# Scan of 16-row blocks to 64x64 inverses: two of four heads sent crosswise through the matmul array, and powers plus the unit matrix in place of the additions

## The chip, the cores and the metric

One core of one Trainium2 chip. The metric is the device time of one execution in microseconds (us), of three runs the median.

## The reference, cut to what matters

The program is a whole two-block language-model layer in fp32 (norm, MLA attention with 8 heads, an RWKV-7 branch with a forward and a backward scan, gated merge, FFN; then a GLA block and a second FFN). The change touches only the RWKV-7 scans:

```python
def wkv7_scan(r, w, k, v, a, b, reverse):
    def step(state, inp):
        r_t, w_t, k_t, v_t, a_t, b_t = inp
        sa = jnp.einsum('bhvk,bhk->bhv', state, a_t)
        state = (state * w_t[:, :, None, :] + sa[..., None] * b_t[:, :, None, :]
                 + v_t[..., None] * k_t[:, :, None, :])
        return state, jnp.einsum('bhvk,bhk->bhv', state, r_t)
...
    fwd = direction(dlo_f, glo_f, w0[0], w2[0], g2[0], False)
    bwd = direction(dlo_b, glo_b, w0[1], w2[1], g2[1], True)
```

1024 steps, 8 heads of width 64, once forward and once backward.

## The kernel before

Each direction d (0 forward, 1 backward) walks 8 tiles i of 128 time steps. Within a tile the recurrence becomes matrix algebra: for every head a strictly triangular 128x128 matrix has to be inverted (I minus it). It is cut into halves of 64 steps, which lie on partitions 0 to 63 and 64 to 127 (`ROWS`), so that each head has two 64x64 triangles to invert. Four heads are worked on together (a group, `u` = 0 or 1): 8 tiles x 2 directions x 2 = 32 groups. Each triangle is cut into 16-row blocks; inside the blocks the inverse is the product (I+D)(I+D^2)(I+D^4)(I+D^8), and two further steps (H1/X5 with `G1`, H2/T64 with `G2`) put 16-row blocks together to 32 and 64. All operands are fp32; one fp32 matmul is two records in the trace (transposes are one).

**Steps of a group.** `scan_pe`, `scan_ve`, `scan_ae` and `scan_ge` are generators of TensorE, VectorE, ScalarE and GpSimd; each `yield` ends a step, and a group has 13 (`STEPS`). On PE: An (products of `ART` and `BT`; with four tiles of the array), D2, X2 and D4, X3 and D8, X4, H1, X5, H2, T64, V and Y, B, U, O and S; the masked products M go with the D2 and D8 steps (`kinds`). In D2 to H2 `diag` makes one 64x64 matmul per head and half, with operands and result in the same half: half 0 uses the array's quarter (rows 0-63, columns 0-63), half 1 the quarter (64-127, 64-127); the other two quarters have no work. Evacuation: ScalarE copies D2, D4, D8, H1; VectorE adds X2, X3, X4, X5 to the X before.

**Order.** `scans` interleaves the two scans and the attention of the other branch (`att_pe` and so on), one step of each in turn (a round), scan 0 being 7 steps ahead:

```python
s0, s1, at_ = scan(e, 0), scan(e, 1), att_and_loads()
for _ in range(7):
    next(s0)
    next(at_)
interleave(s0, s1, at_)
```

The attention's steps are the scores of a 128-row tile (two 96x128x512 matmuls into two PSUM banks; VectorE takes the maximum, ScalarE `Exp` at L1144, which frees the banks), the transposes of the tile before (eight, two banks), and every second time the product with v. After 64 tiles it is over and the two scans go on alone. All engines work their instructions in program order.

**PSUM.** Eight banks are handed out in a ring by `take`; a pair (`n=2`) begins at an even bank, and a bank is skipped for that if need be. Before PE writes a bank it waits for whoever read the bank's last contents (`frees`). A group takes An, Y, O as pairs and D2, four M, X2, D4, X3, D8, X4, H1, X5, H2, T64, V, B, U, S as single banks, 23 in all.

`state` (its matmuls are the ones with `lax`, L354) writes O and Y from the state matrix: 8 matmuls of 64x64 that go round all four quarters of the array.

Of the kernel before, what the change touches and what calls it, by code (L numbers as in the profile page):

```python
# [235 lines left out]
def program(nc, a, out):  # L236
    ctx = ExitStack()
    with ctx:
# [946 lines left out]
        def scan_memory(d):  # L1185
# [9 lines left out]
            def heads(n):  # L1195
                return part(n).rearrange("p (h n) -> p h n", h=4)
# [14 lines left out]
            c.D8, c.XA, c.XB = [heads(256) for _ in range(3)]  # L1211
# [16 lines left out]
        def hv(b, n=512):  # L1228
            return v3(ps[:, b, 0:n], 4)

        def two(b):

            return ps[:, b, :].rearrange("p (a h n) -> p a h n", a=2, h=4)
# [39 lines left out]
        def scan_pe(pe, d):  # L1273
# [9 lines left out]

            def kinds(i, u, q):
# [18 lines left out]
            for i in range(8):  # L1303
# [13 lines left out]
                for u in range(2):  # L1317
                    b = take(pe, PEs, "An", i, u, n=2)
                    pe.wait_ge(*at(VEs, "T", i, 2))
                    for q in range(2):  # L1320
                        p = 2 * u + q
                        for js in ROWS:
                            for n in range(2):
                                for j, rows in enumerate(ROWS):
                                    at_, bt = c.ART[rows, p, 0, js], c.BT[rows, p, js]
                                    x = mm(pe, ps[js, b + j, 128 * n + 64 * q:128 * n + 64 * q + 64], bt if n else at_,
                                           at_ if n else bt, True, True)
                    x.then_inc(*pe.sig(PEs, "An", i, u))
                    yield
                    b = take(pe, PEs, "D2", i, u)  # L1330
                    pe.wait_ge(*at(VEs, "D1", i, u, 1))
                    diag(b, 0, c.D1[:, 1], c.D1[:, 0])
                    diag(b, 256, c.D1[:, 0], c.D1[:, 1]).then_inc(*pe.sig(PEs, "D2", i, u))
# [19 lines left out]
                    b = take(pe, PEs, "X4", i, u)  # L1353
                    pe.wait_ge(*at(AEs, "D8", i, u))
                    pe.wait_ge(*at(VEs, "X3", i, u))
                    diag(b, 0, c.D8, c.XA).then_inc(*pe.sig(PEs, "X4", i, u))
                    yield
                    b = take(pe, PEs, "H1", i, u)
                    pe.wait_ge(*at(VEs, "X4", i, u))
                    pe.wait_ge(*at(GEs, "G2", i, u))  # L1360
                    for h in range(4):
                        for js in ROWS:
                            mm(pe, ps[js, b, 64 * h:64 * h + 64], c.X1[js, 1, h, :], ident[js, js], True, True)
                    diag(b, 256, c.G1, c.X1[:, 1]).then_inc(*pe.sig(PEs, "H1", i, u))
                    yield
                    b = take(pe, PEs, "X5", i, u)
                    pe.wait_ge(*at(AEs, "H1", i, u))
                    diag(b, 0, c.X1[:, 2], c.X1[:, 0])
                    diag(b, 256, c.X1[:, 0], c.X1[:, 2]).then_inc(*pe.sig(PEs, "X5", i, u))
                    yield  # L1370
                    b = take(pe, PEs, "H2", i, u)
                    pe.wait_ge(*at(VEs, "X5", i, u))
# [80 lines left out]
        def scan_ve(ve, d):  # L1453
# [11 lines left out]

            def less_own(i):
# [33 lines left out]
            for i in range(8):  # L1500
# [11 lines left out]
                for u in range(2):  # L1512
                    b = bank(PEs, "An", i, u)
                    ve.wait_ge(*at(PEs, "An", i, u))
                    for n, mask in enumerate((c.dN, c.dT)):
                        tt(ve, even_odd(c.D1[:, n]), ps[:, b:b + 2, 128 * n:128 * n + 128].rearrange("p j (q n) -> p j q n", q=2),
                           mask.unsqueeze(1).unsqueeze(1).broadcast_to([P, 2, 2, 64]), ALU.mult).then_inc(
                            *ve.sig(VEs, "D1", i, u, n))
                    yield
                    masked(i, u, 0)  # L1520
                    yield
                    ve.wait_ge(*at(PEs, "X2", i, u))
                    tt(ve, c.XB, hv(bank(PEs, "X2", i, u), 256), c.XA, ALU.add).then_inc(*done("X2", i, u))
                    yield
                    ve.wait_ge(*at(PEs, "X3", i, u))
                    ve.wait_ge(*at(VEs, "X2", i, u))
                    tt(ve, c.XA, hv(bank(PEs, "X3", i, u), 256), c.XB, ALU.add).then_inc(*done("X3", i, u))
                    masked(i, u, 1)
                    yield
                    ve.wait_ge(*at(PEs, "X4", i, u))  # L1530
                    tt(ve, c.X1[:, 1], hv(bank(PEs, "X4", i, u), 256), c.XA, ALU.add).then_inc(*done("X4", i, u))
                    yield
                    yield
                    ve.wait_ge(*at(PEs, "X5", i, u))
                    tt(ve, c.X2, two(bank(PEs, "X5", i, u)), c.X1[:, 0:2], ALU.add).then_inc(*done("X5", i, u))
# [4 lines left out]
                    ve.wait_ge(*at(VEs, "X5", i, u))  # L1540
# [25 lines left out]
        def scan_ae(ae, d):  # L1566
# [6 lines left out]

            def exps(i):
# [11 lines left out]
            for i in range(8):  # L1586
# [1418 lines left out]
```

## Time and profile before

| | |
|---|---|
| median of 3 runs | 3591.54 us (3588.69 to 3591.72) |
| profiled execution | 3593.16 us, span 3591.4 us |
| PE (matmuls) busy | 3414.7 us, 95% of the span |
| VectorE, ScalarE, GpSimd busy | 1714.2, 1107.4, 324.1 us |
| scans beside the attention | about 573 to 1185 us of the span |
| scans alone | about 1185 to 1341 us |

The span is the time between the first and the last recorded instruction; the execution's own time is 1.8 us more. A line number like L355 is that of a helper (L355: every plain matmul, L354: matmuls of `state` and `rows_by`, L358: transposes, L361: ScalarE copies, L364: VectorE and GpSimd operations on two tensors), so groups are told apart by the names of the tiles. Scan 0's tiles lie in AR and EX, scan 1's in X, W and AR; `HT` and `W` also hold the attention's.

### The profile page before, as it was taken

To read this page: it belongs to the slowest core of one execution; us is meant where nothing else is said; L and a number is where in the kernel's file an instruction comes from. 1 tells how busy PE (TensorE), PEld (TensorE's weight loads), DVE (VectorE), ACT (ScalarE), POOL (GpSimd) and SP (SyncE) were. 2 spreads that over 40 slices of the span, in tenths; PEclk is the share of its full clock that TensorE was granted. 3 is DMA by queue.
4 is the path that set the end of the run, shared out by engine and by line. 5 is a ranking of instruction groups with operands and counts; after the bars stand their busy time and mean duration, and the time that the engine had idled before them with its cause. 6 is when DMAs were issued, how large, how long until landed. Compare 5 with 4: busy or idle time off the path is not lost.

```text
span 3591.4 us, 61000 instructions
## 1 busy us (share of the span) xinstructions
PE 3414.7 (95%) x27176; PEld 2714.1 (76%) x27176; DVE 1714.2 (48%) x2528; ACT 1107.4 (31%) x1797; POOL 324.1 (9%) x342
## 2 busy tenths in 40 slices
PE   8989999999999996999999999899899999999998
PEld 7678776777777883487888888687677788888877
DVE  4353555665555566554335434552454522352235
ACT  4323324444444330132124212433232311241124
POOL 1232241111111222000000000001000000000000
PEclk9999999999999998999999999999899999999999
DMA  3241252212111204421112211232003111121113
GB/s 138 70 143 50 83 187 81 66 39 63 38 58 46 100 12 144 139 90 42 47 47 94 77 47 47 100 107 96 18 30 106 65 53 47 59 100 59 47 65 106
DMA packets 89974, 269.82 MB, mean 75 GB/s; under 512 B 11552, under 2 KB 12080, under 8 KB 89712
## 3 DMA queue, kind: packets, MB, share of 16 engines
q1 hardware_dynamic: 78960, 230.26, 19.6%
q0 software_dynamic: 10752, 35.66, 2.9%
q8 instruction: 215, 3.52, 0.4%
q14 instruction: 47, 0.39, 0.0%
HBM read 219.73 MB, written 46.14 MB: 74 GB/s over the span
## 4 chain that ended last, share of the span: by engine, by line
PE 83%; DVE 10%; ACT 3%; issue 2%; DMA 1%; SPq 0%; POOL 0%; DVEq 0%; ACTq 0%
PE ps L355 78%; PE ps L354 3%; PE ps L358 2%; DVE SM L375 2%; DVE X L364 2%; DVE AR L364 1%; ACT HT L1144 1%; DVE HT L368 1%; DVE W L364 1%; ACT WS L361 0%; DVE HL L364 0%; ACT W L2043 0%; DVE EX L364 0%; DVE WS L364 0%; DMA qk_d<-AR 0%
## 5 line engine op out<-in xcount | busy, mean ns | idle before, releaser
L355 PE MATMUL ps<-HH,WS 128*128 128x512 f32 (+1 forms) x3232 | 1000.6, 391 | 0.0
L355 PEld LDWEIGHTS ps<-HH,WS 128*128 128x128 f32 (+1 forms) x3232 | 607.2, 188 | 129.7
L355 PE MATMUL ps<-HL,WS 128*128 128x512 f32 x1616 | 639.1, 395 | 7.1 <-DVE HL L364 6.9
L364 DVE TENSOR_TENSOR WS<-W,WS 128x1024 fp32r<-128x1024 f32 x244 | 299.4, 1227 | 635.1 <-ACT WS L361 635.1
L361 ACT ACTIVATE WS<-W 128x1024 fp32r<-128x1024 f32 x244 | 256.6, 1052 | 891.8 <-PE ps L355 885.1
L355 PE MATMUL ps<-WS,SA 128*128 128x512 f32 x2112 | 491.3, 394 | 24.6 <-DVE SA L364 22.4
L355 PEld LDWEIGHTS ps<-WS,SA 128*128 128x128 f32 x2112 | 400.9, 191 | 112.1 <-issue 26.8
L355 PEld LDWEIGHTS ps<-HL,WS 128*128 128x128 f32 x1616 | 303.8, 188 | 73.0 <-issue 7.6
L355 PE MATMUL ps<-AR 64*64 64x64 f32 (+2 forms) x4928 | 202.3, 241 | 10.0 <-ACT AR L361 4.2
L355 PE MATMUL ps<-HL,HI 128*128 128x512 f32 (+1 forms) x512 | 208.3, 407 | 3.7 <-POOL WL L364 2.8
L355 PE MATMUL ps<-WS,HH 128*128 128x512 f32 x640 | 203.7, 394 | 7.5 <-DVE HL L364 5.4
L364 DVE TENSOR_TENSOR SA<-HA,SA 128x512 fp32r<-128x512 f32 x176 | 120.9, 691 | 184.8 <-ACT SA L361 184.8
L355 PE MATMUL ps<-WS,HL 128*128 128x512 f32 x576 | 206.9, 392 | 0.8 <-DVE X L364 0.8
L355 PE MATMUL ps<-HH,HI 128*128 128x512 f32 (+1 forms) x512 | 205.6, 401 | 0.0
L355 PE MATMUL ps<-HH,WL 128*128 128x512 f32 (+1 forms) x512 | 204.6, 400 | 0.0
L355 PEld LDWEIGHTS ps<-AR 64*64 64x64 f32 (+1 forms) x4928 | 161.7, 135 | 56.7 <-issue 35.6
L361 ACT ACTIVATE SA<-HA 128x512 fp32r<-128x512 f32 x176 | 110.3, 631 | 281.7 <-PE ps L355 252.9
L355 PE MATMUL ps<-HT 96*128 96x512 f32 (+1 forms) x384 | 187.0, 619 | 0.6 <-DMA HT<-v_d 0.5
L361 ACT ACTIVATE AR<-ps 128x512 f32<-128x512 f32 (+4 forms) x240 | 115.3, 493 | 130.2 <-PE ps L355 92.0
L364 DVE TENSOR_TENSOR HA<-HA,ps 128x512 f32<-128x512 f32 x88 | 60.4, 687 | 184.9 <-PE ps L355 184.1
L355 PEld LDWEIGHTS ps<-WS,HH 128*128 128x128 f32 x640 | 120.8, 189 | 33.7 <-issue 5.6
L1144 ACT ACTIVATE HT<-ps,SM 128x1024 f32<-128x1024 f32 x64 | 71.3, 1114 | 214.7 <-DVE SM L368 214.7
(287 smaller groups left out, 4442.1 us busy)
## 6 DMA issues: line engine op xcount, KB each, us to landing
W<-in_w_fd SPq DMA_DIRECT2D x88, 512.0 KB, 3.3
AR<-rw_d SPq DMA_DIRECT2D x104, 256.0 KB, 4.0
W<-in_w_fg SPq DMA_DIRECT2D x44, 512.0 KB, 3.3
W<-in_w_fu SPq DMA_DIRECT2D x44, 512.0 KB, 3.3
W<-in_w_tok SPq DMA_DIRECT2D x24, 512.0 KB, 3.3
rw_d<-X POOLq DMA_DIRECT2D x40, 256.0 KB, 3.3
X<-in_x SPq DMA_DIRECT2D x16, 512.0 KB, 5.5
W<-in_w_g SPq DMA_DIRECT2D x16, 512.0 KB, 3.7
```

What stands on the lines that cost most here:

```text
L354: return pe.e.matmul(o, l, r, start=start, stop=stop, skip_group_check=True)
L355: return pe.e.matmul(o, l, r, start=start, stop=stop)
L358: return pe.e.transpose(o, i, ident)
L361: return e.e.activation(o, x, ACT.Copy)
L364: return e.e.tensor_tensor(o, x, y, op)
L368: return e.e.tensor_scalar(o, x, s1, None, o1)
L375: return e.e.tensor_reduce(o, x, AX.X, op)
L1144: ae.e.activation(APB[i % 2], ps[:, b:b + 2, :].rearrange("p a b -> p (a b)"), ACT.Exp, bias=sm(264 + i % 4, 1), scale=SCALE, accum_out=sm ...
```

## The change

`cross` takes the place of `diag` from D2 to X5. Heads 0 and 1 stay in their halves; of heads 2 and 3 the operands of half z give a result in half 1-z, in a bank of its own. So each of these steps now writes two banks and its matmuls go round all four quarters; heads 2 and 3 change halves at every step, and the step pattern is such that operands meet in the same half. For this An makes a third product for heads 2 and 3 into the other half (4 more matmuls a group), and VectorE masks it into `XA` (`D1`, 2).

X + D X is computed as (I + D) X: VectorE makes `DI` = D + I from the D2, D4, D8 results (`and_one`), PE multiplies with `DI`, and the X results are copied by ScalarE. `D8` alone is no longer kept. H1's addition goes the same way (`X1[2]` = product + I), so that X5 needs no addition. As both engines read the same bank, VectorE's `and_one` waits for ScalarE's copy of the same step (of the last copy from these banks). GpSimd's addition for `XA` is two instructions of half the size.

Per group the matmuls number 20 instead of 16 in An, and 96 in D2 to X5 as before (16+8+16+8+8+8+16+16 before; 16+24+16+8+16+16 now), all 96 crosswise. The banks: An, D2, D4, D8, X4, H1, X5, Y, O as pairs and four M, H2, T64, V, B, U, S as single ones, 28 a group, besides those that are skipped.

```diff
+            def cross(b, c0, lhs, rhs):
+
+                for m in range(2):
+                    for h in (m, 2 + m):
+                        for z in range(2):
+                            o = ROWS[1 - z if h > 1 else z]
+                            x = mm(pe, ps[o, b + h // 2, c0 + 64 * m:c0 + 64 * m + 64], lhs[ROWS[z], h, :], rhs[ROWS[z], h, :],
+                                   True, True)
                 return x
...
-                        for js in ROWS:
-                            for n in range(2):
+                        for n in range(2 + q):
+                            for z, js in enumerate(ROWS):
                                 for j, rows in enumerate(ROWS):
...
-                    b = take(pe, PEs, "X2", i, u)
+                    b = take(pe, PEs, "D4", i, u, n=2)
                     pe.wait_ge(*at(AEs, "D2", i, u))
+                    cross(b, 0, c.D2[:, 1], c.D2[:, 0])
+                    cross(b, 128, c.D2[:, 0], c.D2[:, 1])
                     pe.wait_ge(*at(GEs, "X", i, u))
-                    diag(b, 0, c.D2[:, 0], c.XA).then_inc(*pe.sig(PEs, "X2", i, u))
-                    b = take(pe, PEs, "D4", i, u)
-                    diag(b, 0, c.D2[:, 1], c.D2[:, 0])
-                    diag(b, 256, c.D2[:, 0], c.D2[:, 1]).then_inc(*pe.sig(PEs, "D4", i, u))
-                    yield
-                    b = take(pe, PEs, "X3", i, u)
+                    pe.wait_ge(*at(VEs, "D2", i, u))
+                    cross(b, 256, c.DI, c.XA).then_inc(*pe.sig(PEs, "D4", i, u))
+                    yield
+                    b = take(pe, PEs, "D8", i, u, n=2)
                     pe.wait_ge(*at(AEs, "D4", i, u))
-                    pe.wait_ge(*at(VEs, "X2", i, u))
-                    diag(b, 0, c.D4[:, 0], c.XB).then_inc(*pe.sig(PEs, "X3", i, u))
-                    b = take(pe, PEs, "D8", i, u)
-                    diag(b, 0, c.D4[:, 1], c.D4[:, 0]).then_inc(*pe.sig(PEs, "D8", i, u))
+                    cross(b, 0, c.D4[:, 1], c.D4[:, 0])
+                    pe.wait_ge(*at(VEs, "D4", i, u))
+                    cross(b, 128, c.DI, c.XB).then_inc(*pe.sig(PEs, "D8", i, u))
                     kinds(i, u, 1)
...
+            def and_one(nm, i, u, o, c0):
+
+                ve.wait_ge(*at(PEs, nm, i, u))
+                ve.wait_ge(*at(AEs, {"D4": "X2", "D8": "X3"}.get(nm, nm), i, u))
+                tt(ve, in_pairs(o), heads_of(bank(PEs, nm, i, u), c0), cst["I64"].unsqueeze(1).unsqueeze(1).broadcast_to([P, 2, 2, 64]),
+                   ALU.add).then_inc(*done(nm, i, u))
...
-                    copy(c.D4, two(bank(PEs, "D4", i, u)), "D4", i, u)
-                    yield
-                    copy(c.D8, hv(bank(PEs, "D8", i, u), 256), "D8", i, u)
-                    yield
-                    yield
-                    copy(c.X1[:, 0::2], two(bank(PEs, "H1", i, u)), "H1", i, u)
-                    yield
+                    both(c.D4, "D4", i, u)
+                    one(c.XB, "X2", "D4", 256, i, u)
+                    yield
+                    one(c.XA, "X3", "D8", 128, i, u)
+                    yield
+                    copy(in_pairs(c.X1[:, 1]), heads_of(bank(PEs, "X4", i, u), 0), "X4", i, u)
+                    yield
+                    one(c.X1[:, 0], "H1", "H1", 0, i, u)
+                    yield
+                    both(c.X2, "X5", i, u)
                     yield
```

How the instructions stand. First ScalarE while the scans are alone, from the copy of scan 0's H2 to the next copies of scan 1's H1. Before (scan 0: `AR 128x256` H2, `EX` V, Y, U, O; scan 1: `AR 128x2x2x64` An, `X 128x512` D2 and D4, `AR 128x256` D8, `AR 128x2x256` H1):

```order
L361 ACTIVATE AR<-ps 128x256
L361 ACTIVATE AR<-ps 128x2x2x64
L361 ACTIVATE X<-ps 128x512
L361 ACTIVATE EX<-ps 64x256
L361 ACTIVATE EX<-ps 128x2x2x64
L361 ACTIVATE X<-ps 128x512
L361 ACTIVATE AR<-ps 128x256
L361 ACTIVATE EX<-ps 128x256
L361 ACTIVATE EX<-ps 128x2x2x64
L361 ACTIVATE AR<-ps 128x2x256
```

The same place of the change (`X 128x2x2x128` are D2 and D4, the two `AR 128x256` together XB and XA, the next `AR 128x256` X4, the last H1):

```order
L361 ACTIVATE AR<-ps 128x256
L361 ACTIVATE AR<-ps 128x2x2x64
L361 ACTIVATE X<-ps 128x2x2x128
L361 ACTIVATE EX<-ps 64x256
L361 ACTIVATE EX<-ps 128x2x2x64
L361 ACTIVATE X<-ps 128x2x2x128
L361 ACTIVATE AR<-ps 128x256 x2
L361 ACTIVATE EX<-ps 128x256
L361 ACTIVATE AR<-ps 128x256
L361 ACTIVATE EX<-ps 128x2x2x64
L361 ACTIVATE AR<-ps 128x256
```

The copy of D8 is gone, those of XB, XA and X4 have come, and H1's copy is half as wide.

Second VectorE, scan 0's first group beside the attention. Before (`128x2x2x64` the masks of An, `128x512` the masks of M, `128x256 x2` X2 and X3; the rows between are the attention's):

```order
L364 TENSOR_TENSOR AR<-ps,CS 128x2x2x64 x2
L364 TENSOR_TENSOR AR<-ps,CS 128x512 x2
L1119 RECIPROCAL SM<-SM 128x1
L368 TENSOR_SCALAR HT<-HT,SM 128x1024
L375 TENSOR_REDUCE SM<-ps 128x1
L368 TENSOR_SCALAR SM<-SM 128x1
L364 TENSOR_TENSOR AR<-ps,AR 128x256 x2
L364 TENSOR_TENSOR AR<-ps,CS 128x512 x2
```

and with the change:

```order
L364 TENSOR_TENSOR AR<-ps,CS 128x2x2x64 x2
L364 TENSOR_TENSOR AR<-ps,CS 128x128
L364 TENSOR_TENSOR AR<-ps,CS 128x256
L364 TENSOR_TENSOR AR<-ps,CS 128x512 x2
L1119 RECIPROCAL SM<-SM 128x1
L368 TENSOR_SCALAR HT<-HT,SM 128x1024
L375 TENSOR_REDUCE SM<-ps 128x1
L368 TENSOR_SCALAR SM<-SM 128x1
L364 TENSOR_TENSOR AR<-ps,CS 128x256 x2
L364 TENSOR_TENSOR AR<-ps,CS 128x512 x2
```

One small mask has come, and an `and_one` (`AR<-ps,CS 128x256`) now stands ahead of the masks of M as well.

## Rows read from the trace of the kernel before

**Rows 1.** The page's first parts: span, and busy time of each engine

```profile
span 3591.4 us, 61000 instructions
PE 3414.7 (95%) x27176; PEld 2714.1 (76%) x27176; DVE 1714.2 (48%) x2528; ACT 1107.4 (31%) x1797; POOL 324.1 (9%) x342
```

**Rows 2.** Busy time by stretch: scans with attention, scans alone

```profile
core 0: us, PE busy (x) PEld busy (x) DVE busy (x) ACT busy (x) POOL busy (x), PEclk, DMA share, GB/s
573.00:1185.00 612.00, 583.27 (x11140) 456.36 (x11138) 363.89 (x683) 256.04 (x542) 93.55 (x111) 1.00 0.16 50
1185.00:1341.00 156.00, 146.80 (x4045) 133.40 (x4040) 94.69 (x187) 52.61 (x114) 35.39 (x42) 1.00 0.19 64
```

**Rows 3.** Timeline of PE: `state`, then X4 of scan 1 (`diag`)

```profile
start us, us, engine line op out<-in xcount [idle before <-releaser]
760.37 0.46 PE L354 MATMUL ps<-EX,AR 64*64 64x64 f32 x16
...
761.84 0.68 PE L355 MATMUL ps<-AR 64*64 64x64 f32 x16
```

**Rows 4.** What PE waited for, 573 to 1185 us

```profile
engine line waited for: us in total, times, longest us
PE ps L355 <- ACT AR L361: 7.7, 7, 1.6
PE ps L358 <- ACT W L361: 4.5, 4, 1.4
PE ps L358 <- ACT EX L361: 4.3, 5, 0.9
PE ps L355 <- ACT HT L1144: 2.9, 5, 0.6
```

**Rows 5.** Timeline, one round of scores and its release

```profile
1039.53 1.98 PE L355 MATMUL ps<-HT 96*128 96x512 f32 x4
...
1041.55 1.23 DVE L375 TENSOR_REDUCE SM<-ps 128x1 f32<-128x1024 f32 x1 [1.55 <-PE ps L355]
...
1042.81 0.15 DVE L368 TENSOR_SCALAR SM<-SM 128x1 f32<-128x1 f32 x1
...
1043.00 1.11 ACT L1144 ACTIVATE HT<-ps,SM 128x1024 f32<-128x1024 f32 x1 [2.76 <-DVE SM L368]
...
1043.67 1.24 PE L358 MATMUL ps<-CS,HT 128*128 128x128 f32 x8
...
1044.10 0.37 ACT L361 ACTIVATE AR<-ps 128x256 f32<-128x256 f32 x1
...
1044.26 0.42 PEld L358 LDWEIGHTS ps<-CS,HT 128*128 128x128 f32 x4 [0.17 <-ACT HT L1144]
```

**Rows 6.** Groups of instructions by form, 573 to 1341 us

```profile
line engine op names shapes xcount | busy us, mean ns | idle before us <-releasers
L361 ACT ACTIVATE AR<-ps 128x512 f32<-128x512 f32 x75 | 44.7, 597 | 43.4 <-PE ps L355 37.6 <-PE ps L358 5.8
L361 ACT ACTIVATE AR<-ps 128x256 f32<-128x256 f32 x93 | 35.0, 383 | 39.7 <-PE ps L355 22.1 <-DVE X L364 8.9 <-DVE AR L364 8.6
L364 DVE TENSOR_TENSOR AR<-ps,AR 128x256 f32<-128x256 f32 x93 | 39.2, 422 | 68.8 <-PE ps L355 68.8
L364 DVE TENSOR_TENSOR X<-ps,AR 128x512 f32<-128x512 f32 x7 | 4.8, 692 | 4.4 <-PE ps L355 4.4
L364 DVE TENSOR_TENSOR EX<-ps,EX 128x128 f32<-128x128 f32 x16 | 4.6, 288 | 14.8 <-PE ps L354 14.8
L364 POOL TENSOR_TENSOR AR<-AR,CS 128x256 f32<-128x256 f32 x77 | 56.9, 761 | 153.8 <-DVE AR L364 151.3 <-ACT AR L361 2.0
```

**Rows 7.** Timeline, scans alone: H1, its copy, then X5 and more

```profile
1242.45 0.68 PE L355 MATMUL ps<-CS,AR 64*64 64x64 f32 x16
1242.97 1.16 PE L355 MATMUL ps<-AR 64*64 64x64 f32 x48
...
1243.65 0.60 ACT L361 ACTIVATE AR<-ps 128x512 f32<-128x512 f32 x1 [1.08 <-PE ps L355]
...
1244.39 2.95 PE L355 MATMUL ps<-AR 64*64 64x64 f32 x80 [0.26 <-ACT AR L361]
```

More of the change, by code:

```diff
@@ L1210, in scan_memory @@
             c.An, c.G1, c.G2 = [heads(256) for _ in range(3)]
-            c.D8, c.XA, c.XB = [heads(256) for _ in range(3)]
+            c.DI, c.XA, c.XB = [heads(256) for _ in range(3)]
+            c.eye = cst["I64"].unsqueeze(1).broadcast_to([P, 4, 64])
             c.X1, c.X2 = pair(3), pair(2)
@@ L1229, in hv, with crossed, heads_of, in_pairs @@
             return v3(ps[:, b, 0:n], 4)
-        def two(b):
-            return ps[:, b, :].rearrange("p (a h n) -> p a h n", a=2, h=4)
+        def crossed(b, c0, n=128):
+            return ps[:, b:b + 2, c0:c0 + n]
+        def heads_of(b, c0):
+            return crossed(b, c0).rearrange("p g (m n) -> p g m n", m=2)
+        def in_pairs(ap):
+            return ap.rearrange("p (g m) n -> p g m n", g=2)
         def by_parity(b):
@@ L1329, in scan_pe @@
                     yield
-                    b = take(pe, PEs, "D2", i, u)
+                    b = take(pe, PEs, "D2", i, u, n=2)
                     pe.wait_ge(*at(VEs, "D1", i, u, 1))
-                    diag(b, 0, c.D1[:, 1], c.D1[:, 0])
-                    diag(b, 256, c.D1[:, 0], c.D1[:, 1]).then_inc(*pe.sig(PEs, "D2", i, u))
+                    cross(b, 0, c.D1[:, 1], c.D1[:, 0])
+                    cross(b, 128, c.D1[:, 0], c.D1[:, 1]).then_inc(*pe.sig(PEs, "D2", i, u))
                     pe.wait_ge(*at(AEs, "T", i, 3))
@@ L1355, in scan_pe @@
-                    pe.wait_ge(*at(VEs, "X3", i, u))
-                    diag(b, 0, c.D8, c.XA).then_inc(*pe.sig(PEs, "X4", i, u))
+                    b = take(pe, PEs, "X4", i, u, n=2)
+                    pe.wait_ge(*at(AEs, "X3", i, u))
+                    pe.wait_ge(*at(VEs, "D8", i, u))
+                    cross(b, 0, c.DI, c.XA).then_inc(*pe.sig(PEs, "X4", i, u))
                     yield
-                    b = take(pe, PEs, "H1", i, u)
-                    pe.wait_ge(*at(VEs, "X4", i, u))
+                    b = take(pe, PEs, "H1", i, u, n=2)
@@ L1360, in scan_pe @@
+                    pe.wait_ge(*at(AEs, "X4", i, u))
+                    cross(b, 0, c.X1[:, 1], c.eye)
                     pe.wait_ge(*at(GEs, "G2", i, u))
[L1361 to L1364, printed above, removed]
+                    cross(b, 128, c.G1, c.X1[:, 1]).then_inc(*pe.sig(PEs, "H1", i, u))
@@ L1365, in scan_pe @@
                     yield
-                    b = take(pe, PEs, "X5", i, u)
+                    b = take(pe, PEs, "X5", i, u, n=2)
                     pe.wait_ge(*at(AEs, "H1", i, u))
-                    diag(b, 0, c.X1[:, 2], c.X1[:, 0])
-                    diag(b, 256, c.X1[:, 0], c.X1[:, 2]).then_inc(*pe.sig(PEs, "X5", i, u))
+                    pe.wait_ge(*at(VEs, "H1", i, u))
+                    cross(b, 0, c.X1[:, 2], c.X1[:, 0])
+                    cross(b, 128, c.X1[:, 0], c.X1[:, 2]).then_inc(*pe.sig(PEs, "X5", i, u))
@@ L1572, in copy, with both, one @@
                 cp(ae, o, x).then_inc(*ae.sig(AEs, nm, i, u, frees=(PEs, nm, i, u)))
+            def both(o, nm, i, u):
+                ae.wait_ge(*at(PEs, nm, i, u))
+                cp(ae, o.rearrange("p a (g m) n -> p g a (m n)", g=2),
+                   crossed(bank(PEs, nm, i, u), 0, 256).rearrange("p g (a k) -> p g a k", a=2)).then_inc(
+                    *ae.sig(AEs, nm, i, u, frees=(PEs, nm, i, u)))
+            def one(o, nm, of, c0, i, u):
+                ae.wait_ge(*at(PEs, of, i, u))
+                cp(ae, in_pairs(o), heads_of(bank(PEs, of, i, u), c0)).then_inc(
+                    *ae.sig(AEs, nm, i, u, frees=(PEs, of, i, u)))
             def exps(i):
@@ L1593, in scan_ae @@
                 for u in range(2):
-                    ae.wait_ge(*at(VEs, "D1", i, u, 1))
+                    ae.wait_ge(*at(VEs, "D1", i, u, 2))
                     copy(even_odd(c.An), by_parity(bank(PEs, "An", i, u)), "An", i, u)
                     yield
-                    copy(c.D2, two(bank(PEs, "D2", i, u)), "D2", i, u)
+                    both(c.D2, "D2", i, u)
                     yield
@@ L1647, in scan_ge @@
                 for u in range(2):
-                    ge.wait_ge(*at(VEs, "D1", i, u, 1))
-                    tt(ge, c.XA, c.D1[:, 1], bc(cst["I64"], 4), ALU.add).then_inc(*ge.sig(GEs, "X", i, u))
+                    ge.wait_ge(*at(VEs, "D1", i, u, 2))
+                    for g, src_ in enumerate((c.D1[:, 1, 0:2, :], c.XA[:, 2:4, :])):
+                        x = tt(ge, c.XA[:, 2 * g:2 * g + 2, :], src_, bc(cst["I64"], 2), ALU.add)
+                    x.then_inc(*ge.sig(GEs, "X", i, u))
                     ge.wait_ge(*at(AEs, "An", i, u))
```

25 lines of the change are left out of this document (11 added, 14 removed).

## Prediction

> **What bounds the kernel now.** I read the page first [rows 1]: PE is busy for 95% of the span, every other engine for less than half. Only work that leaves PE's stream, or time in which PE waits, can move the end. All the change touches lies between about 573 and 1341 us, so I then read that stretch in its two parts [rows 2]: with the attention PE is busy for 583 of 612 us, alone for 147 of 156 us; the other engines have room (ScalarE 256 of 612, VectorE 364 of 612). The busy share hides two things, and the next views show them. First, PE's pace: 16 records of `state`, which goes round four quarters of the array, take 0.46 us, 16 records of a `diag` step, which uses two, take 0.68 us [rows 3]. Less the 0.22 us that the last record itself takes, that is 0.016 and 0.031 us a record. Second, how near PE already is to waiting: beside the attention the waits add up to some 28 us over all rows of that view, the longest four of which are shown [rows 4], and where scans run alone X5 waited 0.26 us for the copy of H1 [rows 7]. So PE bounds, with little slack behind it.
>
> **What the change takes away.** 96 matmuls a group x 32 groups x 2 records = 6,144 records go from two quarters to four: 6,144 x 0.0147 us (the difference of the two paces, [rows 3]) = 90 us. An's 4 more matmuls are 256 records x 0.016 = 4 us more; its new order rotates through the quarters a little better, so I take +3. On PE alone: **-87 us**.
>
> What I weigh against it is a rule of the Trainium skill. The row shows one `state` block of 8 matmuls, two of them on each quarter and neighbours sharing row half or column half, at half of `diag`'s time per record. The skill's page "TensorE: Matmul & The Clock Gate" (Part 3, packing small matmuls) says that a weight load overlaps matmuls in flight only where the row group differs. By that rule two quarters on the same row half would not overlap, the 90 us would be nil, and this is a rival below. The trace disagrees with it as far as `state` goes.
>
> **What it puts on the other engines.** VectorE: before, three additions of 0.42 us and one of 0.69 us a group, 1.95 us; now four `and_one` of 0.42 and one mask of 0.29 us, 1.97 us [rows 6]: nothing. ScalarE: three copies of 0.60 and one of 0.38, 2.18 us; now three of 0.60 and four of 0.38, 3.32 us [rows 6]: 1.14 us a group more, 25 us in the attention's stretch, where it is idle for 356 us: hidden as a sum, not as a place in line. GpSimd: one addition of 0.76 us becomes two, which lie between half of that and the whole; they have 2 us and more until D4's third product reads them, so nothing, and if PE came to them early at most 0.4 us a group. DMAs and their queues are not touched.
>
> **What becomes late.** Four places; the first two are large.
>
> (a) The release of the scores' banks. From the end of the score matmuls (1041.5 us) to the end of `Exp` (1044.1) 2.6 us pass: reduce 1.23, scale 0.15, Exp 1.11 and the hand-overs [rows 5]. Here PE had been held at the transposes' second half already (0.17 us). With 23 banks a group the ring comes back to one of the scores' banks after 2.2 to 3.9 us of PE work, 3.3 us in the middle (counted along the code, matmuls x pace). With 28 banks, skipped ones, and the work halved in those steps, it is 1.5 to 3.4 us, 2.2 in the middle: nearly every one of the 64 score blocks is now short, by 0.5 us on average, 30 us in all against 3. Where scan 0's next step comes first, it also wants ScalarE, and its copy stands behind the Exp: it is ready 3.0 us (0.37 or 0.60 more) after the scores, on top of about 2.3 us of work, so short by 0.8 to 0.9. That holds for half of the 60 rounds: 28 us; the other half wait for the bank, 24 us. Together 52 us, where now it is some 25 us. **+27 us**.
>
> (b) O and S. By the new ring, in 17 of the 32 groups S takes a bank that O, right ahead of it, has just filled, and waits for ScalarE's copy of O: the last matmul 0.22, the copy 0.38 and hand-overs, 0.7 us. In the others there is mostly another step between. 17 x 0.7 = **+12 us**; before, this pair never met.
>
> (c) Scans alone. The longest wait of a step was copy or addition; now D4 to D8 is copy 0.60, copy 0.38, `and_one` 0.42, with tail and hand-overs 1.8 us from PE's end to the second half of D8, and the other scan covers 0.9 to 1.4 us of it and D8's first half 0.23. H1 to X5 is 1.1 us against 0.5 to 0.9 of cover, An to D2 1.0 against 0.5 to 0.9, X4 to H1 0.65 against 0.3. The shortfalls of a pair of groups (one of each scan) add up to 2.8 us, against 1.8 us now (156 less 147 us over five pairs, [rows 2]). For five pairs: **+5 us**.
>
> (d) VectorE in the attention's rounds. `and_one` now waits for a ScalarE copy that stands behind Exp, so scan 1's VectorE step and the next reduce stand behind it. Between nothing (PE has other work) and 0.42 + 0.38 us for each of 60 rounds, 48 us. I take **+8 us**, near the lower end, since rounds with the transposes and with the product with v follow and have 1.0 and 1.9 us of PE work of their own.
>
> Sum: -87 + 27 + 12 + 5 + 8 = -35 us, against the profiled execution of 3593.2 us: 3558 us. That execution lies 1.6 us above the median; taken off, **3556 us**, 1.0% faster.
>
> The skill's page "TensorEngine Tiling (Array Packing)" (PSUM Bottleneck) warns that tiling speeds up TensorE and not the evacuation. The trace can't show that for this change yet; (a) and (b) are what it would mean here.
>
> **Rivals.**
>
> R1: the waits are hidden. If VectorE and ScalarE keep up, -70 to -87 us, 3505 to 3521 us. For it: both engines are idle for most of the time [rows 2]. Against it: they are idle because they wait in line, and PE is already held by Exp in the row shown [rows 5]. Chance 0.13.
>
> R2, slower: the chain through Exp, copy and `and_one` becomes the clock of the attention's stretch. Price: (d) at its upper end, 48 us, and in addition the same queueing once more at each D8 and X5 of the stretch, 22 groups x 2 x 1.0 us (0.60 + 0.42) = 44 us; -87 + 27 + 12 + 5 + 48 + 44 = +49 at most, +5 to +30 us likely, 3597 to 3622 us. It decides from the point where a round's PE work beside the scores (2.8 us) is below the 4.2 us that Exp, copy and `and_one` take for the late cases in more than one round out of two and a half. Chance 0.10.
>
> R3: four quarters are no faster in these steps than two. Then the 90 us are nil and the longer chains remain, as the cover is as before, some +5 to +15 us, 3597 to 3607 us. Against it stands the pace of `state` [rows 3]. The skill's rule quoted above would give this. Chance 0.04.
>
> R4: gain and waits cancel, 3585 to 3598 us. Chance 0.10.
>
> **The numbers.** My forecast, with (a) to (d) between half and one and a half of what I take, gives -9 to -61 us, 3531 to 3583 us, chance 0.63. The range reaches half into R1 and into R4: 3517 to 3592. About 0.2% (7 us) is what a measurement of this kernel can tell from no change. Faster by more: 0.63 + 0.13 and a little of R4, 0.80; same: 0.07; slower: 0.13.
>
> **What would show it.** PE's records for D2 to X5 should stand 0.015 us apart, 16 in 0.46 us; their busy time in the two stretches falls together by 50 to 90 us. PE's waits for ScalarE (L1144 and L361) beside the attention should come to 60 to 90 us instead of 28. S should wait for the copy of O in half the groups. The stretch alone should be near 130 us instead of 156, the one with the attention near 600 instead of 612. I am wrong if the records stand 0.03 apart (R3), if the waits stay below 40 us (R1), or if the stretch with the attention gets longer (R2).

## The result and the profile after

The changed kernel takes 3617.21 us, median of 4 runs (3612.48 to 3624.22), beside 3591.63 us for the kernel before on the same chip. The ratio is 1.0073, with a 95% interval of 1.0051 to 1.0094: 0.7% slower, 26 us. The forecast was 3556 us, and the range (to 3592) does not hold the result; rival R2 had the size, and part of the mechanism.

The first parts of the page of the changed kernel, answering to [rows 1]:

```profile
span 3611.8 us, 61777 instructions
PE 3366.4 (93%) x27432; PEld 2645.9 (73%) x27432; DVE 1707.3 (47%) x2560; ACT 1141.4 (32%) x1893; POOL 330.3 (9%) x374
```

PE is busy for 48 us less, and yet the span of this execution is 20 us longer. To see where, I cut the scans' stretch at the places where the attention and the scans end. They are 1185.7 and 1351.7 us before, 1219.4 and 1377.8 us after: 26.1 us are lost by the end of the scans (behind it this execution runs 6 us shorter). The part with the attention is 34 us longer, the scans alone are 8 us shorter (158 against 166 us). That the part with the attention gets longer is the sign which the prediction had set for R2. Busy time by stretch, of the kernel before (as [rows 2], up to the end of the scans):

```profile
core 0: us, PE busy (x) PEld busy (x) DVE busy (x) ACT busy (x) POOL busy (x), PEclk, DMA share, GB/s
563.00:1352.00 789.00, 748.73 (x15475) 604.75 (x15476) 467.89 (x888) 316.26 (x672) 130.65 (x154) 1.00 0.17 52
```

The same of the changed kernel, whole and in its two parts:

```profile
core 0: us, PE busy (x) PEld busy (x) DVE busy (x) ACT busy (x) POOL busy (x), PEclk, DMA share, GB/s
563.00:1378.00 815.00, 705.79 (x15723) 540.97 (x15724) 459.87 (x919) 350.06 (x769) 136.57 (x185) 0.96 0.16 50
...
573.00:1219.00 646.00, 558.26 (x11331) 416.78 (x11331) 360.74 (x706) 280.41 (x610) 98.02 (x134) 0.97 0.16 48
1219.00:1368.00 149.00, 131.17 (x4128) 111.70 (x4124) 90.26 (x195) 61.83 (x142) 37.19 (x51) 0.98 0.20 65
```

The length less PE's busy time is its idle time: 789 - 748.7 = 40 us before, 815 - 705.8 = 109 us now. So **69 us of idle time** have come for 43 us less of work. And PEclk, the granted clock, is 0.96 where it was 1.00. Three things are to be explained: the matmuls' gain, the waits, the clock.

**The matmuls are faster, nearly as forecast.** Timeline of PE in the changed kernel, X5 of scan 0, all 16 matmuls (32 records) crosswise:

```profile
1049.02 0.69 PE L355 MATMUL ps<-AR 64*64 64x64 f32 x32 [2.25 <-DVE AR L364]
```

0.69 less the last record's 0.22 is 0.47 us for 32 records, 0.015 us a record; in [rows 3] `diag` needed 0.031. From the start of a block's first record to that of its last (medians over the blocks at full clock without a wait), D2 falls from 0.93 to 0.48 us, X2 and D4 together from 1.34 to 0.71, X3 and D8 together from 0.88 to 0.48, X4 from 0.46 to 0.24, H1 and X5 from 0.93 to 0.48 each: 2.6 us a group, less 0.05 for An, about **82 us** in 32 groups. The rule of the Trainium skill ("TensorE: Matmul & The Clock Gate", Part 3), by which a weight load overlaps only where the row group differs, does not hold here. In `diag` as in `cross` (and in `state`) each matmul stands on the other row half than the one before, so by that rule the two would keep the same pace. They do not: with the column halves changing too, a record takes half the time. The prediction says that neighbours in `state` share a row half or a column half; by the code they never share a row half.

**The waits.** What PE waited for, 563 to 1378 us, the longest rows:

```profile
engine line waited for: us in total, times, longest us
PE ps L358 <- ACT HT L1144: 18.0, 21, 2.6
PE ps L355 <- DVE AR L364: 16.6, 34, 2.3
PE ps L354 <- ACT EX L361: 14.1, 9, 2.4
PE ps L355 <- ACT AR L361: 13.1, 12, 2.0
PE ps L354 <- ACT W L361: 12.5, 8, 3.4
PE ps L354 <- ACT HT L1144: 7.0, 4, 1.8
PE ps L355 <- ACT HT L1144: 5.3, 6, 1.2
```

Against [rows 4] three kinds are new. L1144 (Exp) holds the scores' banks; `EX L361` and `W L361` at L354 are S waiting for the copy of O, 9 and 8 times, 17 in all; `DVE AR L364` is mostly X5 and D8 waiting for `and_one`. Followed through the program step by step, PE's waits for semaphores come to 124 us against 47: for Exp 34.5 against 5.5 us, S for O's copy 28.0 against none, X5 for H1's `and_one` 11.4 against none. This count comes out above PE's idle time; the view, which counts idle time alone, gives 109 against 41 us, for Exp 30.3 against 5.4, for S 26.6.

How S waits is seen in one round. Timeline, changed kernel: scores, O, then S:

```profile
start us, us, engine line op out<-in xcount [idle before <-releaser]
1007.12 1.98 PE L355 MATMUL ps<-HT 96*128 96x512 f32 x4
...
1009.03 0.69 PE L354 MATMUL ps<-EX,AR 128*64 128x64 f32 x16
1009.14 1.23 DVE L375 TENSOR_REDUCE SM<-ps 128x1 f32<-128x1024 f32 x1 [0.50 <-PE ps L355]
1010.40 0.15 DVE L368 TENSOR_SCALAR SM<-SM 128x1 f32<-128x1 f32 x1
1010.59 1.11 ACT L1144 ACTIVATE HT<-ps,SM 128x1024 f32<-128x1024 f32 x1 [2.96 <-DVE SM L368]
...
1011.70 0.37 ACT L361 ACTIVATE EX<-ps 128x256 f32<-128x256 f32 x1
1012.12 0.20 PEld L354 LDWEIGHTS ps<-EX,AR 128*64 128x64 f32 x4 [2.54 <-ACT EX L361]
```

O is done at 1009.7, ScalarE is idle, and still the copy comes only at 1011.70. It stands behind Exp in ScalarE's program, and Exp waits for VectorE's maximum. S, right behind O on PE, waits 2.4 us here, where I had counted 0.7.

X5's wait has the same root. Timeline, changed kernel, scores, then H1's evacuation:

```profile
1045.43 1.21 DVE L375 TENSOR_REDUCE SM<-ps 128x1 f32<-128x1024 f32 x1
...
1046.87 1.11 ACT L1144 ACTIVATE HT<-ps,SM 128x1024 f32<-128x1024 f32 x1 [4.66 <-DVE SM L368]
...
1047.97 0.37 ACT L361 ACTIVATE AR<-ps 128x256 f32<-128x256 f32 x1
...
1048.45 0.42 DVE L364 TENSOR_TENSOR AR<-ps,CS 128x256 f32<-128x256 f32 x1 [1.62 <-ACT AR L361]
```

Maximum, Exp, copy, `and_one`, then X5 (1049.02, the row above): four instructions on two engines in line.

**The clock.** Busy time by stretch of the changed kernel around the wait of S shown above, which ended at 1012.12:

```profile
1008.00:1012.00 4.00, 1.72 (x19) 0.74 (x17) 2.02 (x3) 1.41 (x3) 0.00 (x0) 1.00 0.02 4
1012.00:1016.00 4.00, 3.88 (x60) 3.69 (x61) 1.86 (x3) 1.49 (x4) 2.56 (x2) 0.63 0.00 0
1016.00:1020.00 4.00, 4.00 (x76) 3.59 (x75) 2.15 (x4) 1.63 (x4) 1.04 (x1) 0.94 0.14 50
```

Within 1 us of the wait's end the granted clock falls to its lower level (1.2 GHz) for some 3.4 us. In the scans' stretch this happens 14 times, 58 us in all; in the kernel before once, 7 us, at its end. 13 of the 14 begin within 1.4 us of the end of a wait of 1.8 us or more, most of them behind it and two 0.2 to 0.3 us ahead of it. Ten other waits of over 1.7 us have none behind them.

### The profile page after: what moved, and what is told of

It reads as the page before. It is cut to its first block, busy times and chain, and to the rows that moved or that the text cites. A ratio compares the mean times of both kernels' runs of the same rounds, so it can differ in the third digit from the quotient of the medians.

```text
span 3611.8 us, 61777 instructions
## 1 busy us (share of the span) xinstructions
PE 3366.4 (93%) x27432; PEld 2645.9 (73%) x27432; DVE 1707.3 (47%) x2560; ACT 1141.4 (32%) x1893; POOL 330.3 (9%) x374
## 4 chain that ended last, share of the span: by engine, by line
PE 76%; DVE 13%; ACT 6%; issue 3%; DMA 1%; SPq 0%; POOL 0%; DVEq 0%; ACTq 0%
PE ps L355 72%; DVE SM L375 3%; PE ps L354 3%; DVE X L364 2%; DVE AR L364 2%; PE ps L358 2%; ACT HT L1144 2%; DVE HT L368 1%; ACT AR L361 1%; ACT WS L361 0%; DVE W L364 0%; ACT W L2081 0%; DVE WS L364 0%; DVE HL L364 0%; DMA qk_d<-AR 0%
## 5 line engine op out<-in xcount | busy, mean ns | idle before, releaser
L364 DVE TENSOR_TENSOR WS<-W,WS 128x1024 fp32r<-128x1024 f32 x244 | 299.6, 1228 | 632.5 <-ACT WS L361 632.5
L361 ACT ACTIVATE WS<-W 128x1024 fp32r<-128x1024 f32 x244 | 256.8, 1053 | 887.0 <-PE ps L355 880.3
L364 DVE TENSOR_TENSOR SA<-HA,SA 128x512 fp32r<-128x512 f32 x176 | 120.9, 692 | 184.8 <-ACT SA L361 184.8
L361 ACT ACTIVATE SA<-HA 128x512 fp32r<-128x512 f32 x176 | 110.6, 632 | 281.4 <-PE ps L355 252.7
L364 DVE TENSOR_TENSOR AR<-ps,CS 128x256 f32<-128x256 f32 (+2 forms) x256 | 112.0, 469 | 184.2 <-ACT AR L361 172.5
L355 PE MATMUL ps<-AR 64*64 64x64 f32 (+2 forms) x5568 | 168.8, 243 | 27.5 <-DVE AR L364 16.6
L355 PEld LDWEIGHTS ps<-AR 64*64 64x64 f32 (+1 forms) x5568 | 120.7, 137 | 81.9 <-issue 39.7
L361 ACT ACTIVATE AR<-ps 128x256 f32<-128x256 f32 (+4 forms) x304 | 131.1, 448 | 131.4 <-PE ps L355 82.5
L364 DVE TENSOR_TENSOR HA<-HA,ps 128x512 f32<-128x512 f32 x88 | 60.5, 688 | 184.2 <-PE ps L355 183.4
```

The costliest lines, as they stand in the source:

```text
L355: return pe.e.matmul(o, l, r, start=start, stop=stop)
L361: return e.e.activation(o, x, ACT.Copy)
L364: return e.e.tensor_tensor(o, x, y, op)
```

## The experiments

"Slow" is the time at the lower clock. Ratios are to the kernel before on the same chip (4 runs of it beside the changed kernel, 11 to 23 beside the others, median 3591.6 to 3594.0 us); the experiments ran on several chips, so small differences between them are better read from the ratios. The other columns are of one profiled execution each. Length, busy and idle are PE's from 563 us to the end of the scans, slow and the waits for the same stretch.

| kernel | median us | ratio, 95% | length | busy | idle | slow | S for O | for Exp |
|---|---|---|---|---|---|---|---|---|
| before | 3591.6 | | 789 | 749 | 40 | 7 | 0 | 5.5 |
| changed | 3617.2 | 1.0051-1.0094 | 815 | 706 | 109 | 58 | 28.0 | 34.5 |
| e1 | 3651.7 | 1.0152-1.0178 | 853 | 775 | 78 | 34 | 26.3 | 19.7 |
| e2 | 3626.8 | 1.0082-1.0108 | 825 | 765 | 60 | 37 | 23.8 | 18.7 |
| e3 | 3603.4 | 1.0018-1.0042 | 806 | 706 | 100 | 65 | 0 | 35.5 |
| e4 | 3606.5 | 1.0024-1.0050 | 805 | 722 | 83 | 34 | 26.1 | 24.6 |
| e5 | 3616.5 | 1.0044-1.0069 | 813 | 757 | 56 | 17 | | |
| e6 | 3600.6 | 1.0008-1.0025 | 797 | 730 | 67 | 21 | | |
| e7 | 3594.5 | 0.9997-1.0015 | 799 | 721 | 78 | 48 | | |
| e8 | 3623.2 | 1.0067-1.0091 | 821 | 776 | 45 | 27 | | |
| e9 | 3578.6 | 0.9949-0.9977 | 780 | 726 | 54 | 21 | | |
| e10 | 3588.0 | 0.9973-0.9994 | 783 | 711 | 72 | 31 | | |
| e11 | 3589.0 | 0.9976-1.0001 | 785 | 713 | 72 | 31 | | |
| e12 | 3610.8 | 1.0039-1.0066 | 807 | 753 | 54 | 14 | 0 | |
| e13 | 3618.9 | 1.0057-1.0081 | 816 | 725 | 91 | 54 | 8.4 | |
| e14 | 3639.1 | 1.0114-1.0140 | 830 | 727 | 103 | 68 | 28.0 | |
| e15 | 3620.0 | 1.0062-1.0088 | 818 | 774 | 44 | 14 | 6.4 | |

### e1: no crossing, all else as changed

```diff
-                            o = ROWS[1 - z if h > 1 else z]
+                            o = ROWS[z]
```
(and the same in An's third product)

> The changed kernel with every head kept in its own half: the same matmuls, banks, copies and waits, but D2 to X5 on two quarters. Where PE's time alone counts it is 70 to 90 us slower than the changed kernel's 3617 us. If the waits that came with the change (PE waits 124 us in the scans' stretch, 47 before) fill up what the faster matmuls save, the slow matmuls cover these waits again: waits of 50 to 70 us, the clock at full speed in the stretch, and a time within 20 us of the changed kernel's. If four quarters gave nothing in place, the time and the waits would both be the changed kernel's.

3651.7 us, 34 us slower than the changed kernel and 60 us slower than the one before. That lies between the two cases expected, and the clock did not stay at full speed (34 us slow). So crossing by itself is a gain, but of 34 us. PE's busy time, less half of the slow time, is 758 us here and 677 us in the changed kernel: 81 us of work go, and idle time rises from 78 to 109 us, slow time from 34 to 58 us. Banks, chain and An's third product together cost 60 us. Of the 26 us of busy time that e1 has more than the kernel before, 14 are the clock and 4 An; some 9 us are left. In part they are the ends of matmuls, which count as busy when PE stops behind them: PE stops 97 times here, 58 times in the kernel before (pauses over 0.06 us).

### e2: the kernel before with the banks of the change

```diff
-                    b = take(pe, PEs, "D2", i, u)
+                    b = take(pe, PEs, "D2", i, u, n=2)
```
(and the same for X4, H1, X5)

> The kernel before, with D2, X4, H1 and X5 taken as pairs of banks, so the ring goes on 28 banks a group instead of 24; nothing else. If the pressure on the banks is what costs (terms a and b), the waits for Exp's and O's banks grow by 10 to 25 us and the time goes to 3600 to 3617 us. If it is the chain of copies and additions, or the clock, it stays within 5 us of 3592 us.

No instruction is added, and the kernel is 35 us slower, more than the 8 to 25 us expected. What PE waited for in e2, 563 to 1388 us:

```profile
PE ps L354 <- ACT EX L361: 14.1, 9, 2.4
PE ps L355 <- ACT AR L361: 9.3, 11, 1.6
PE ps L354 <- ACT W L361: 8.4, 8, 1.9
PE ps L355 <- ACT HT L1144: 6.9, 9, 1.4
```

The first and third row are S, again 17 times. And PE's busy time has grown by 16 us at the same instructions:

```profile
563.00:1388.00 825.00, 764.94 (x15474) 616.89 (x15474) 468.73 (x887) 320.27 (x674) 130.69 (x154) 0.98 0.16 50
```

That is the clock: 30 us more at half speed than in the kernel before, half of which is 15 us. Idle time (+20) and clock (+16) make up the 36 us of the stretch.

### e3 and e4: one cause taken out of the changed kernel

```diff
                     b = take(pe, PEs, "U", i, u)
+                    bs_ = plan.next_place(BANKS, (PEs, "S", i, u))[1]
...
-                    b = take(pe, PEs, "S", i, u)
+                    b = bs_
+                    for tok in plan.releases((PEs, "S", i, u)):
+                        pe.wait_ge(*tok)
```

> The changed kernel, with the bank of S taken right behind that of U in the ring, so it is never the one that O has just filled. The 28 us of waits of S for the copy of O go. If such waits lie on the path one for one, the time falls by 20 to 30 us to 3587 to 3597 us, more if the half-speed stretches get rarer. If they only delay what would wait later anyway (the next step for Exp or a copy), it falls by under 10 us.

3603.4 us, 14 us faster, less than the 28 us of the wait. Slow time did not fall (65 against 58 us), and 4 of the 13 falls stand behind no wait of 1.7 us or more. A new wait takes part of the old one's place: the shifted ring brings H1 to O's banks, 8 times, 10.5 us, most of this row (in the changed kernel it had 4.0 us):

```profile
PE ps L355 <- ACT EX L361: 13.6, 7, 2.0
```

In e4 PE adds I and X itself, and `and_one` is gone:

```diff
+            def plus(b, c0, lhs, rhs, one_):
...
+                    for k, l_, r_ in ((0, lhs, rhs), (1, c.eye, one_)):
...
-                    pe.wait_ge(*at(VEs, "D2", i, u))
-                    cross(b, 256, c.DI, c.XA).then_inc(*pe.sig(PEs, "D4", i, u))
+                    plus(b, 256, c.D2[:, 0], c.XA, c.XA).then_inc(*pe.sig(PEs, "D4", i, u))
```
(and so for X3, X4 and the second product of H1)

> The changed kernel, with I and X added by PE into PSUM (8 more small matmuls on I in X2, X3, X4 and H1, 32 a group) and no and_one: one ScalarE copy ends each step. PE has 32 x 32 x 2 records x 0.015 us = 30 us more. If VectorE's place behind the copy (and_one) is what costs, waits of PE for D4, D8, H1 fall by 15 to 25 us, the attention's reduce comes earlier, and the time is within 15 us of 3617 us or below it. If it is not, the time is 20 to 35 us longer: 3637 to 3652 us.

3606.5 us: 11 us faster, though PE has about 30 us more to do (busy time +16 us, with 24 us less at half speed). The chain is a cost of its own.

### e5: the chain without the banks

The changed kernel's steps with `diag`'s layout: D2, D8, X4, H1, X5 write one bank each, nothing crosses.

> The changed kernel's chain (and_one behind ScalarE's copy, X copied) without crossing and without its banks: D2, D8, X4, H1, X5 in one bank each, 23 banks a group. If the banks (+35 us by e2) and the chain add up to the 60 us that e1 lost against the kernel before, the chain alone costs 25 us: 3610 to 3625 us. If the chain costs only where the banks are late as well, it is within 8 us of 3592 us.

3616.5 us, 23 us above the median of the kernel before beside it. By the ratios e2 costs 34, e5 20 and e1 59 us: banks and chain are two costs that nearly add. The largest rows of what PE waited for in e5 (its helper lines stand two further down):

```profile
PE ps L357 <- DVE AR L366: 10.9, 17, 1.9
PE ps L357 <- ACT AR L363: 10.2, 12, 1.5
```

### e6 to e8: fewer banks, less crossing, both remedies

e6 crosses D2 and D4 alone and takes 24 banks; e7 is e3 and e4 together; e8 is e7 with e6's banks. e8 does not give the right result: part of its additions of I and X is missing from it. Its instructions are all there, so its time can be read; two sums are open in one bank at the same time, but no run shows that this is why.

> The changed kernel with crossing in D2 and D4 alone; D8, X4, H1, X5 stay in their halves and take one bank each, so 24 banks a group as before the change. Faster matmuls by 32 x 1.0 us = 32 us only, instead of 75. If the four banks more are what turns the gain into a loss, this comes below the changed kernel: about 3617 - 35 + 43 = 3625 us if banks cost the full 35 us, less if waits shrink with the shorter ring as well; under 3592 us only if the chain's 25 us are hidden too. If banks did not matter it would be 3617 + 40 = 3657 us.

> e3 and e4 together: crossing everywhere, PE adds I and X in PSUM, no and_one, and S's bank is taken behind U's. If the two gains (14 and 11 us) are of different waits they add: 3588 to 3596 us. If one wait only takes the place of the other, it stays at 3600 to 3607 us.

> As e7, but with crossing in D2 and D4 alone and one bank each for D8, X4, H1, X5: 24 banks a group. PE has 43 us more than e7. If the banks' pressure is worth over 43 us it is faster than e7, otherwise 0 to 40 us slower; the waits for Exp's banks should fall from some 25 to under 10 us either way, and the clock stay at full speed in the stretch.

e6 is 17 us faster than the changed kernel, though it gives up some 43 us of faster matmuls: idle time 67 instead of 109 us, slow time 21 instead of 58. It was expected at about 3625 us, so the shorter ring gives back more than the 35 us that e2 had cost. e7 has both gains (23 us against 25 for the sum) and stands level with the kernel before. e8 is 29 us slower than e7, the second of the two cases expected. Idle time fell by 33 us and slow time by 21, but PE's busy time rose by 55: besides the products, PE's own additions then run on two quarters as well, which the expectation left out. With `and_one` gone the faster matmuls are worth more than the banks.

### e9: cross only where no chain grows

The kernel before, with the change in An, D2, D4 and X2 only. From X3 on `diag` and VectorE's additions are back.

```diff
+                    bx = take(pe, PEs, "X3", i, u)
+                    b = take(pe, PEs, "D8", i, u)
                     pe.wait_ge(*at(AEs, "D4", i, u))
-                    cross(b, 0, c.D4[:, 1], c.D4[:, 0])
-                    pe.wait_ge(*at(VEs, "D4", i, u))
-                    cross(b, 128, c.DI, c.XB).then_inc(*pe.sig(PEs, "D8", i, u))
+                    diag(b, 0, c.D4[:, 1], c.D4[:, 0]).then_inc(*pe.sig(PEs, "D8", i, u))
+                    pe.wait_ge(*at(AEs, "X2", i, u))
+                    diag(bx, 0, c.D4[:, 0], c.XB).then_inc(*pe.sig(PEs, "X3", i, u))
```

> The kernel before with crossing only where no chain gets longer: An, D2 and D4 with X2 cross (one and_one, behind D2); from X3 on everything is as before the change, VectorE's additions too. 25 banks a group by the ring (before 24). PE has 32 x (0.38 + 0.63) - 2 = 30 us less. If banks and chain were what ate the gain, most of the 30 us is kept: 3562 to 3580 us. If any faster matmul in this stretch is given back in waits, whatever the banks and the chain, it is 3585 to 3600 us.

3578.6 us, ratio 0.9963 (0.9949 to 0.9977): **faster than both**. Of 30 us of faster matmuls 13 to 15 are kept (by the ratio and by the medians). Its row:

```profile
563.00:1343.00 780.00, 725.72 (x15723) 576.30 (x15724) 468.58 (x919) 327.16 (x707) 135.34 (x185) 0.99 0.17 53
```

Against the kernel before: busy -23, idle +14 (this execution lies 5.5 us above its median). What PE waited for shows what is left of the banks' cost:

```profile
PE ps L355 <- ACT AR L361: 12.4, 14, 2.0
PE ps L358 <- ACT HT L1144: 6.1, 12, 0.8
PE ps L354 <- ACT HT L1144: 5.2, 4, 1.8
```

> e9, and H1 and X5 cross too, with I added by PE in H1 (no and_one) and both evacuated by ScalarE: two banks more (27). PE has 32 x 0.62 = 20 us less than e9, two pairs more of banks cost up to 20 us. Theory of banks: within 10 us of e9. Theory of waits in proportion to PE's gain: the same. Without a cost of banks: 3545 to 3560 us.

> e10 with the bank of S taken behind U's. Where S meets O's banks in e10, 5 to 15 us faster than e10; where it doesn't, the same, or slower if the shifted ring brings O and another step together, as H1 in e3.

e10 is 8 to 9 us slower than e9: two pairs of banks more, and H1's and X5's evacuation by ScalarE, cost more than crossing H1 and X5 gives. These two costs were not separated. S's place (e11) changes nothing. e10 and e11 have 15 and 13 us less busy time than e9, and 18 us more idle time each.

### e12: e2 with e3's edit

> e2 (the kernel before with 28 banks a group) with the bank of S taken behind U's: it splits e2's 35 us. S waited 24 us for O's copy in e2. If that is the larger part, this is 15 to 25 us below e2's 3627 us; if the waits only move to the next step that meets O or Exp, under 8 us below it.

16 us below e2: somewhat less than half of the banks' cost is S's wait, with the clock behind it. Most of it is the clock. Idle time falls by 6 us only (60 to 54), as H1 now waits for O's banks, five times 1.9 us; slow time falls from 37 to 14 us. Behind those five waits the clock falls once, while in e2 it fell behind six of S's seven waits of 1.8 to 2.4 us.

### e13 to e15: is it the waits that pull the clock down?

```diff
-                    b = take(pe, PEs, "S", i, u)
+                    b = plan.next_place(BANKS, (PEs, "S", i, u))[1]
+                    if b in (bo, bo + 1):
+                        for n in range(24):
+                            mm(pe, ps[ROWS[n % 2], bu, 64 * (n % 8 // 2):64 * (n % 8 // 2) + 64],
+                               c.TT[:, n % 8 // 2, ROWS[n % 2]], c.Y[:, n % 8 // 2, :], True, True)
+                    for tok in plan.releases((PEs, "S", i, u)):
+                        pe.wait_ge(*tok)
```
(e14: `not in`; e15: on e2)

> The changed kernel, with 24 repeated matmuls of U (1.28 us of PE, into U's own bank, whose contents nobody needs any more) ahead of S in the 17 groups where S waits for the copy of O. They stand in time in which PE waits anyway; when the wait ends stays as it was. If the half-speed stretches come from PE standing still for some 2 us, at least 5 of the 14 falls of the clock (those behind S) go, and the time falls by 5 to 12 us, to 3605 to 3612 us, though PE does 22 us more. If the stretches have another cause, they stay, and the time is 0 to 8 us longer (short waits are overfilled).

> The control: the same 24 matmuls in the 15 other groups, where S does not wait. If the fillers cost their PE time: 15 x 1.28 = 19 us more than the changed kernel, 3636 us. If the stretch is bound by the chains rather than by PE, under 10 us more. The falls of the clock should stay about 14.

> e2 with the filler of e13 in its groups where S waits for O: of e2's 8 falls of the clock (37 us at half speed, PE busy 16 us longer at the same instructions) most stand behind such a wait. If the waits make them, slow time falls by half or more, and the time from 3627 us to 3610 to 3620 us. If not, it is the same or up to 8 us longer.

e15 is the clean case. Timeline of PE in e2, the wait of S in one group and what follows:

```profile
1127.07 0.69 PE L354 MATMUL ps<-EX,AR 128*64 128x64 f32 x16
1130.16 0.48 PE L354 MATMUL ps<-EX,AR 128*64 128x64 f32 x4 [2.40 <-ACT EX L361]
...
1131.21 1.12 PE L355 MATMUL ps<-CS,AR 64*64 64x64 f32 x16
```

The same place in e15:

```profile
1127.40 0.69 PE L354 MATMUL ps<-EX,AR 128*64 128x64 f32 x16
1127.91 1.57 PE L355 MATMUL ps<-EX 128*64 128x64 f32 x48
1130.49 0.34 PE L354 MATMUL ps<-EX,AR 128*64 128x64 f32 x4 [1.00 <-ACT EX L361]
...
1131.10 0.68 PE L355 MATMUL ps<-CS,AR 64*64 64x64 f32 x16
```

The second fence's x48 row is the filler. S starts 3.09 us after O in both, but in e2 the next 16 records take 1.12 us and in e15 0.68. Over the stretch the falls go from 8 to 2, none of them behind S, slow time from 37 to 14 us; and though PE issues 22 us more, the time falls by 7 us (the intervals of the two ratios still touch). In the control e14, where the filler stands in groups without the wait, there are 13 falls and 68 us. So in e2 it is PE's standing still that brings the clock down.

In the changed kernel (e13) the falls behind S's waits for O are gone as well, 7 of 14, but others have come behind waits that had none before (11 falls, 54 us slow), and the time is unchanged (+2 us), outside the 3605 to 3612 us expected if the waits were all. It has 13 waits above 1.7 us left where there were 23; e15 has one. Why a fall follows one such wait and not another stays open (e12's five waits say the same), and with it how much of the changed kernel's 58 us any one wait causes.

e14 pays in full: the filler where PE does not wait costs 22 us (19 by the ratios) for 19 us of matmuls. So even the changed kernel is bound by PE's time between the waits.

## Why the prediction was wrong

The steps that failed are the price of (b) and a term that the sum did not have, the clock. The sum was -87 us of work and +52 us of waits. In the stretch, at the same clock, PE's busy time fell by 69 us (745 to 677, each less half of the slow time), idle time rose by 69 us, and the clock cost another 26 us: +26 us. So of the miss of 61 us some 18 lie in the work, 17 in the waits and 26 in the clock. Step by step:

- **Pace, -87 us.** Right in kind (0.015 us a record) and nearly in size: 82 us by the starts, a miss of 5. Busy time shows 69. The other 13 us are in part the ends of matmuls before the new waits (PE stops 136 times against 58) and in part slower neighbouring steps; how they divide is not shown.
- **(a) Scores' banks, +27 us.** The difference held: the waits for Exp rose by 29 us (25 of idle time). (In its working, 30 rounds at 0.8 to 0.9 us are 24 to 27 us, not 28.)
- **(b) O and S, +12 us.** The number of groups was right (17), the price was not: 1.65 us each, 28 us (26.6 of idle time). I had added matmul tail, copy and hand-over, as if ScalarE were free to copy. It was idle, but its next instruction in order was Exp. [Rows 5] shows the same queue, and I had used it in (a) and not here. Miss: 16 us.
- **(c) and (d), +5 and +8 us.** What idle time is left for them is 17 us, and e5, with the chain alone, has 16 us more of it: near the 13 forecast. But the scans alone went from 166 to 158 us, not down by 26.
- **Not in the sum: the clock.** 51 us more at half speed cost about half of that, an estimate that e2 bears out (30 us more, busy time +16). It is the largest single part of the miss.

The sign for the waits was met: PE's waits for ScalarE (L1144 and L361) beside the attention come to 70 us, within the 60 to 90 forecast. R2 (chance 0.10) named the side and the line of instructions (Exp, copy, `and_one`), and its range holds the result, in part by luck. Its price, queueing at each D8 and X5, is not what decided: X5 waited 11 us for `and_one`, D8 10 us for D4's results, 44 us had been put on them, and R2 had no clock either. The banks alone (e2) cost more than the chain alone (e5). R1 falls with 124 us of waits, R3 with the pace, R4 with the size.

The trace of before warned in two ways. Its idle time in the stretch was 40 of 789 us, so any gain of PE had only chains behind it that were already as long. e1 shows how little is then kept: 34 of 81 us. And it shows the second price of a wait, though not within [rows 2], where the clock is 1.00. Where the attention's branch begins, PE waits 3.62 us for VectorE, up to 543.9 us. Timeline of PE, kernel before:

```profile
543.90 1.17 PE L358 MATMUL ps<-CS,AR 128*128 128x128 f32 x8 [3.62 <-DVE AR L364]
```

Busy time by stretch of the kernel before, same place; the granted clock (the third number from the end) falls:

```profile
540.00:544.00 4.00, 0.38 (x2) 0.13 (x2) 1.63 (x3) 3.03 (x5) 0.86 (x2) 1.00 0.90 237
544.00:548.00 4.00, 3.52 (x11) 1.88 (x12) 1.05 (x2) 0.60 (x2) 2.62 (x2) 0.67 0.24 91
548.00:552.00 4.00, 4.00 (x12) 2.61 (x11) 1.98 (x3) 1.21 (x3) 0.00 (x0) 0.50 0.00 0
```

In that whole trace the clock falls 21 times, 14 of them within a wait of more than 2.5 us or within 2 us of its end. What it could not show is that waits of 1.8 to 2.4 us already do it: the stretch had no wait above 1.8 us.

The Trainium skill's page "TensorE: Matmul & The Clock Gate" (A second HAM failure mode: psum-queue depth-cycling) tells of a kernel whose PE pauses between groups while it cycles through banks, and whose clock swings for that. e2 against e15 agrees; in the changed kernel (e13) filling the waits did not lower the time. Its page "PSUM — Partial Sum Buffer" (PSUM bank collisions raise a hardware error) is why `and_one` must stand behind the copy at all: two engines may not read one bank at once. No run here shows that.

## What to carry to other kernels

A bank, a buffer or a slot more per step is a change of its own: try it alone, without the faster code, as in e2, before counting on the gain. Price a wait for an engine by what stands ahead in its program order at that moment, not by whether it is idle. And where PE is the bound, take its waits of some 2 us twice: once for themselves, once for the half-speed stretch that may follow. The trace of before shows such stretches elsewhere in the program even when the part to be changed has none.

## What was not expected of the hardware

- The granted clock fell to its lower level at waits of only 1.8 to 3.4 us, for 3.4 us in most cases and for 6.8 or 10.2 us in some. Over the changed kernel and e2, 20 of 22 falls began within 1.5 us of the end of a wait of 1.8 us or more (in e3 9 of 13, within 1.6 us); filling the waits took them away in e15 and moved them in e13.
- Four 64x64 quarters of the array in turn issue a record every 0.015 us, two quarters in turn only every 0.03 us, though the row half changes from matmul to matmul in both.
